# Leaving the last freed ring slot's load to the next block

## The chip, the cores and the metric

One core of a Trainium2 chip runs the whole program in one launch. The metric is the device time of one execution in microseconds (us). The kernel before took 2956.96 us (median of 3 runs, 2953.3 to 2957.9). Engines are called as in the profile: PE (TensorE matmuls), PEld (TensorE weight loads), DVE (VectorE), ACT (ScalarE), POOL (GpSimd), SP (SyncE). A "q" behind a name means the engine's sequencer: waits, branches, semaphore clears and the issue of DMAs.

## The reference

Two transformer blocks, one behind the other, on x of 256 tokens by 1024 channels, all in float32:

```python
def reference(x, ...):
    x = first_block(x, ...)      # 2 layers: token mixing, then a dense SwiGLU or a mixture of 8 experts
    return second_block(x, ...)  # RWKV-7 + NSA + S5 mixer, convolved FFN, per-layer embedding

def first_block(x, ...):
    for l in range(2):
        x = x + token_mixing(x, ...)          # rmsnorm, x @ w_in, pooling / mLSTM / FoX branches, gates, @ w_out
        h = rmsnorm(x, ffn_norm_g[l])
        x = x + (swiglu(h, ...) if l == 0 else moe_swiglu(h, ...))   # moe: top 2 of 8, 3584 wide
    return rmsnorm(x, final_norm_g)

def second_block(x, p, ...):
    z = rms_norm(h, ...) @ w_in
    mix = concat([rwkv7(z), nsa(z), s5(z)]) @ w_out
    h = h + rms_norm(mix); h = h + rms_norm(conv_ffn(rms_norm(h)))
    return h + sigmoid(h @ w_ple_gate) * rms_norm(p @ w_ple)
```

What matters for this change is only that nearly every product has a weight that is read once from memory, some 530 MB in all, and that the products come in a fixed order.

## The kernel before, in words

**The weight ring.** All big weights are cut into slabs of at most 128 partitions by 4096 floats (2 MB) and listed in `m.plan` in the order in which PE will use them (`plan_slabs`, `plan_experts`, `plan_second`, L183 to L222 and L1169). They pass through a ring of six slots in on-chip memory (`self.slots` is 6; a seventh slot of the tile serves as scratch). Slab i goes into slot i mod 6, so it can be loaded once PE is done with slab i - 6. PE counts the slabs it is done with in the semaphore `slabs_used`: `done_with_slab` (L155) notes a debt, and the next matmul without a signal of its own (L164), or `settle` at the end of the block (L173), pays it. `settle` first waits for the block's last matmul.

**Who loads.** Only SP issues slab loads (`issue`, L135, the DMA is L141). It works through them in order, and for slab i waits until `slabs_used` has reached i - 5. In Python, `self.used` is the number of slabs released up to the point that the program text has reached, and `self.issued` the number of slabs whose load is already written out. Nearly every block's SP program is `m.prefetch(sp)` (L144): issue up to slab `used + 6`, then clear the semaphores that the block before this one used (`clear_last`, L118; the clears are L120). The two pools of semaphores take turns from block to block.

**Blocks.** The program is a row of 51 such blocks, each one `nc.Block()` with a program for each engine. A block ends for all engines together: each drains, POOL gathers them, and releases them all into the next block. In the trace these are the DRAIN and EVENT_SEMAPHORE instructions on the line of the `with nc.Block()` that follows (L405 rmsnorm, L448 projections, L638 local mixers, L783 mLSTM, L898 attention, L999 merge, L1051 gated FFN, L1349 experts, L1592 extra jobs, L2215 NSA projections). The drain stands on the line of the block that ends. Where the SP program is written below the PE program (`rmsnorm`, `projections`, `local_mixers`, `merge`, `gated_ffn`, `experts`, `nsa_project` and others) `self.used` already counts the block's own slabs when `prefetch` is written out; so SP's last wait in such a block is for PE's last release.

**Blocks with loads of their own.** Some blocks have small loads on SP besides the ring. In `rwkv_prepare` (L1766 to L1770), `route`, `nsa_compressed`, `S5.prepare` and `ple` they stand ahead of `m.prefetch(sp)`. In `extra_jobs` (L1594 to L1606), which follows `experts` directly, `m.prefetch(sp)` stands first, and then a loop of as many rounds as a value computed on the chip says (one round here) waits and loads three tiles of 512 KB for PE (gate and up L1604, down L1606).

Of the kernel before, what the change touches and what calls it, by code (L numbers as in the profile page):

```python
# [50 lines left out]
class Signal:  # L51

    def __init__(self, sem):
        self.sem, self.n = sem, 0
# [23 lines left out]
class Machine:  # L79

    def __init__(self, nc, a, ctx):
        self.nc, self.a, self.ctx = nc, a, ctx
        self.names = {}
        self.slots = SLOTS - 1
        sem = lambda name: ctx.enter_context(nc.semaphore(name))
        self.slab_in = [sem(f"slab_in{i}") for i in range(SLOTS)]
        self.slabs_used = sem("slabs_used")
        self.load_in = [sem(f"load_in{i}") for i in range(6)]
        self.pools = [[sem(f"phase{b}_{i}") for i in range(26)] for b in (0, 1)]  # L90
        self.turn = 0
        self.taken = 0
        self.dirty = [0, 0]
        self.plan = []
        self.number = {}
        self.issued = 0
        self.used = 0
        self.owed = 0
        self.ring = self.sb("ring", [P, SLOTS, SLAB])
        self.bank = [ctx.enter_context(nc.psum_tensor(f"bank{i}", [P, 512], F32)) for i in range(8)]  # L100

# [13 lines left out]
    def sem(self):  # L115
        return self.signals(1)[0].sem
# [5 lines left out]
    def end_block(self):  # L122
        self.dirty[self.turn] = self.taken
        self.turn, self.taken = 1 - self.turn, 0

    def add_slab(self, key, src, kt, n):
# [15 lines left out]

    def prefetch(self, sp):  # L144

        self.issue(sp, self.used + self.slots)
        self.clear_last(sp)

    def slab(self, pe, key):
# [2678 lines left out]
```

## Time and profile before

| | |
|---|---|
| runs | 2956.96 us median (2953.3, 2956.96, 2957.9) |
| the profiled execution | 2956.46 us, of which 2954.7 us is the span from the first to the last instruction |
| PE busy | 2548.4 us, 86% of the span |
| PEld / DVE / ACT / POOL busy | 1751.8 / 688.2 / 271.2 / 75.6 us |
| mean granted TensorE clock | 0.903 of full speed |
| memory traffic | 529.67 MB read, mean 181 GB/s |

The profile is of one execution. Busy time is the time in which an engine works, sequencer instructions left out. A row of a timeline gives start, length, engine, line and operation; rows for one line of the source give the number of instructions, their shortest, median and longest duration in ns, and the start of the first and the last.

### The profile page before, as it was taken

The page shows a single profiled execution, that of the slowest core. Times are in us where ns is not written, and L with a number is a line of the kernel's source. Part 1 is how long each engine was busy: PE and PEld are TensorE (multiplying, and loading weights), DVE is VectorE, ACT ScalarE, POOL GpSimd, SP SyncE. Part 2 cuts the span into 40 slices and gives each one's busy share as a digit, 9 for nine tenths or more (in the row PEclk, how much of TensorE's full clock was granted, in tenths as well). Part 3 has the DMA queues.
Part 4 walks back from the last instruction along what each step waited for, and adds up shares of the span by engine and source line. Part 5 has one row for each costly group of instructions (what it writes and reads, how often), then busy time and mean ns, then how long its engine had stood idle before and what let it go on. Part 6 is the DMA issues. An engine that isn't in the chain of part 4 may idle for free. (4 is left out here: it accounts for less than half of the span.)

```text
span 2954.7 us, 43386 instructions
## 1 busy us (share of the span) xinstructions
PE 2548.4 (86%) x19584; PEld 1751.8 (59%) x19584; DVE 688.2 (23%) x1523; ACT 271.2 (9%) x510; POOL 75.6 (3%) x139
## 2 busy tenths in 40 slices
PE   5988989989989899999999999984576755779976
PEld 4766778877667745345354354443475643468865
DVE  1322310013222210101001000112374224533332
ACT  0222100001222010000000000001100001110000
POOL 1000000000000000000000000001000003100000
PEclk9988999999889989999999999997786855889987
DMA  6321424353311649999999999990200310014320
GB/s 223 141 71 43 159 98 171 114 186 118 113 45 46 225 174 382 372 393 389 367 406 374 370 407 373 378 364 22 92 1 1 124 34 0 11 47 171 128 75 15
DMA packets 165222, 533.51 MB, mean 181 GB/s; under 512 B 16012, under 2 KB 31278, under 8 KB 148654
## 3 DMA queue, kind: packets, MB, share of 16 engines
q1 hardware_dynamic: 158944, 529.86, 48.0%
q8 instruction: 154, 2.52, 0.3%
q10 hardware_dynamic: 6094, 0.88, 0.2%
q14 instruction: 30, 0.25, 0.0%
HBM read 529.67 MB, written 1.05 MB: 180 GB/s over the span
## 5 line engine op out<-in xcount | busy, mean ns | idle before, releaser
L160 PE MATMUL bank<-hT,ring 128*128 128x256 f32 x3280 | 752.4, 390 | 55.1 <-PEq L405 23.6
L160 PEld LDWEIGHTS bank<-hT,ring 128*128 128x128 f32 x3280 | 639.6, 196 | 156.8 <-issue 64.7
L160 PE MATMUL bank<-ring,moe_he 128*32 128x512 f32 (+1 forms) x6144 | 579.6, 539 | 0.0
L160 PEld LDWEIGHTS bank<-ring,moe_he 128*32 128x32 f32 x6144 | 199.2, 110 | 375.3 <-issue 373.8
L160 PE MATMUL bank<-ring,moe_actT 128*32 128x256 f32 x5376 | 293.2, 379 | 0.0
L160 PEld LDWEIGHTS bank<-ring,moe_actT 128*32 128x32 f32 x5376 | 174.0, 110 | 116.6 <-issue 3.4
L1552 DVE TENSOR_TENSOR moe_act<-moe_silu,bank 128x512 f32<-128x512 f32 (+1 forms) x48 | 26.9, 616 | 547.6 <-PE bank L160 547.6
L160 PE MATMUL bank<-norm_sq,ones 128*128 128x256 f32 x160 | 58.8, 547 | 51.5 <-ACT norm_sq L408 51.5
L160 PEld LDWEIGHTS bank<-norm_sq,ones 128*128 128x128 f32 x160 | 45.0, 289 | 65.2 <-ACT norm_sq L408 55.4
L160 PE MATMUL bank<-cffn_act,ring 128*128 128x256 f32 x352 | 79.7, 379 | 0.4 <-DVE cffn_act L1151 0.4
L160 PE MATMUL bank<-ffn_act,ring 128*128 128x256 f32 x352 | 79.4, 379 | 0.0
L160 PEld LDWEIGHTS bank<-cffn_act,ring 128*128 128x128 f32 x352 | 66.8, 190 | 9.8 <-DVE cffn_act L1151 0.8
L160 PEld LDWEIGHTS bank<-ffn_act,ring 128*128 128x128 f32 x352 | 66.9, 190 | 9.1
L160 PE MATMUL bank<-ring,hT 128*128 128x512 f32 (+1 forms) x192 | 67.8, 513 | 2.2 <-PEq L448 2.2
L1485 ACT ACTIVATE moe_silu<-bank 128x512 f32<-128x512 f32 (+1 forms) x48 | 22.6, 545 | 415.1 <-PE bank L160 415.1
L1116 DVE TENSOR_TENSOR ffn_act<-ffn_gate,bank 128x256 f32<-128x256 f32 x22 | 9.3, 421 | 216.1 <-ACT ffn_gate L1112 216.1
L160 PE MATMUL bank<-merged,ring 128*128 128x256 f32 x256 | 55.7, 380 | 3.0 <-PEq L999 3.0
L160 PEld LDWEIGHTS bank<-merged,ring 128*128 128x128 f32 x256 | 48.5, 190 | 10.3 <-issue 3.8
L1512 DVE TENSOR_TENSOR xT<-xT,bank 128x512 f32<-128x512 f32 x32 | 19.8, 681 | 147.5 <-PE bank L160 147.5
L160 PEld LDWEIGHTS bank<-ring,hT 128*128 128x128 f32 x192 | 33.2, 201 | 34.9 <-issue 34.9
L1145 DVE TENSOR_SCALAR cffn_cgate<-bank,param 128x256 f32<-128x256 f32 x22 | 12.0, 543 | 147.8 <-PE bank L160 147.8
L1502 DVE COPY moe_ye<-bank 128x256 f32<-128x256 f32 x8 | 3.4, 424 | 152.1 <-PE bank L160 152.1
(595 smaller groups left out, 2168.5 us busy)
## 6 DMA issues: line engine op xcount, KB each, us to landing
ring<-in_moe_w_down SPq DMA_DIRECT2D x56, 2048.0 KB, 14.0
ring<-in_moe_w_gate SPq DMA_DIRECT2D x32, 2048.0 KB, 16.7
ring<-in_moe_w_up SPq DMA_DIRECT2D x32, 2048.0 KB, 9.8
ring<-in_w_in SPq DMA_DIRECT2D x29, 2048.0 KB, 8.0
ring<-in_moe_w_gate SPq DMA_DIRECT2D x32, 1536.0 KB, 8.2
ring<-in_moe_w_up SPq DMA_DIRECT2D x32, 1536.0 KB, 8.5
ring<-in_w_up SPq DMA_DIRECT2D x10, 2048.0 KB, 7.9
ring<-in_w_out SPq DMA_DIRECT2D x6, 2048.0 KB, 7.8
```

Source lines behind the costliest of these rows:

```text
L160: ins = pe.matmul(out, lhsT, rhs, start=start, stop=stop, **kw)
L1116: v.tensor_tensor(act, gate, bank[:, T:2 * T], ALU.mult).then_inc(sg["act"].sem, 1)
L1145: k.step(v.tensor_scalar(to, hu, tap(2, row), bias(row), ALU.mult, ALU.add))
L1485: act.activation(x.sg[:, g, 0:32 * nb], G[g][:, 0:32 * nb], ACT.Silu).then_inc(sg_ready.sem, 1)
L1502: v.tensor_copy(x.ye[:, 2, :], DN[1][:, 0:T]).then_inc(ye_ready.sem, 1)
L1512: ins = v.tensor_tensor(m.xT[:, 2 * cg:2 * cg + 2, :], m.xT[:, 2 * cg:2 * cg + 2, :], SC[cg][:].rearrange("p (c n) -> p c n", c=2), ALU.add)
L1552: v.tensor_tensor(x.act[:, g, 0:32 * nb], x.sg[:, g, 0:32 * nb], U[g][:, 0:32 * nb], ALU.mult)\
```

## The change

`end_block` notes how many slabs had been released when the block ended (`began` for the next one). `prefetch` no longer issues up to `used + 6`: it stops at `used + 5`, but never short of `began + 6`. So a block that releases u slabs (u at least 1) leaves the load that waits for the last of these releases to the next block, whose SP program starts with it; a block that releases none issues all that is open, as before. Where the plan has no more slabs, nothing changes.

```diff
@@ Machine.__init__
         self.owed = 0
+        self.began = 0
@@
     def end_block(self):
         self.dirty[self.turn] = self.taken
         self.turn, self.taken = 1 - self.turn, 0
+        self.began = self.used
@@
     def prefetch(self, sp):
 
-        self.issue(sp, self.used + self.slots)
+        self.issue(sp, max(self.began + self.slots, self.used + self.slots - 1))
         self.clear_last(sp)
```

## Rows read from the trace of the kernel before

**Rows 1.** The profile's page: busy us of each engine, share of the span, instructions

```profile
PE 2548.4 (86%) x19584; PEld 1751.8 (59%) x19584; DVE 688.2 (23%) x1523; ACT 271.2 (9%) x510; POOL 75.6 (3%) x139
```

**Rows 2.** The waits, of SP's queue and of PE: total, times, longest

```profile
SPq L141 <- PE bank L160: 1907.2, 259, 34.7
...
PE bank L1621 <- DMA ring<-in_moe_w_down: 3.2, 1, 3.2
```

**Rows 3.** Line L448 from 380 to 402 us: how a block of projections ends

```profile
L448 DVEq DRAIN  x1: 783/783/783, 400.4 to 400.4; - x1
...
L448 SPq DRAIN  x1: 7/7/7, 401.1 to 401.1; - x1
```

**Rows 4.** The timeline around the same end

```profile
400.38 0.75 DVE L623 TENSOR_TENSOR xT<-xT,bank 128x256 f32<-128x256 f32 x2 [6.16 <-PE bank L160]
400.46 0.37 SPq L141 DMA_DIRECT2D ring<-in_ff_w_down  x1
401.43 1.91 ACT L408 ACTIVATE norm_sq<-xT 128x2048 f32<-128x2048 f32 x1 [65.10 <-PEq L448]
```

**Rows 5.** The timeline from 2594.5 us, and L120 there: the second output projection's end

```profile
2595.07 0.76 DVE L2139 COPY hT<-bank 128x256 f32<-128x256 f32 x2 [6.15 <-PE bank L160]
2595.15 0.37 SPq L141 DMA_DIRECT2D ring<-in_w_down  x1
2596.54 1.91 ACT L408 ACTIVATE norm_sq<-hT 128x2048 f32<-128x2048 f32 x1 [30.46 <-PEq L448]
...
L120 SPq EVENT_SEMAPHORE_RANGE_CLEAR  x15: 25/25/25, 2595.6 to 2596.6; - x15
```

**Rows 6.** The timeline from 2337 us: the end of the NSA projections

```profile
2337.91 0.42 DVE L2174 COPY s_u<-bank 128x256 f32<-128x256 f32 x1 [3.03 <-PE bank L160]
...
2338.99 0.20 POOL L2265 MEMSET swap<- 128x128 f32 x1 [282.73 <-POOLq L2215]
```

**Rows 7.** The timeline from 132.5 us: the end of the local mixers

```profile
133.32 0.60 ACT L695 ACTIVATE fq<-bank 128x512 f32<-128x512 f32 x1 [6.31 <-PE bank L160]
...
134.22 0.68 DVE L787 TENSOR_TENSOR_SCAN run_max<-gi 4x256 f32<-4x256 f32 x1 [10.28 <-PEq L638]
```

**Rows 8.** SP's timeline around attention and merge; the page's landing times

```profile
305.63 0.37 SPq L141 DMA_DIRECT2D ring<-in_w_br_ml  x1
329.98 0.37 SPq L141 DMA_DIRECT2D ring<-in_w_br_fox  x1
336.89 7.28 SPq L141 DMA_DIRECT2D ring<-in_w_out  x2
...
ring<-in_w_in SPq DMA_DIRECT2D x29, 2048.0 KB, 8.0
```

**Rows 9.** The timeline from 1984 us: experts' end and the extra job

```profile
1985.44 0.37 SPq L141 DMA_DIRECT2D ring<-in_w_in  x1
1987.67 2.48 DVE L1512 TENSOR_TENSOR xT<-xT,bank 128x512 f32<-128x512 f32 x4 [3.08 <-PE bank L160]
...
1994.90 1.55 SPq L1604 DMA_DIRECT2D hT<-in_moe_w_up  x1
1996.68 0.39 SPq L1606 DMA_DIRECT2D ring<-in_moe_w_down  x1
...
2002.58 3.84 PE L1621 MATMUL bank<-moe_silu,hT 128*128 128x128 f32 x32 [3.19 <-DMA ring<-in_moe_w_down]
```

**Rows 10.** DMA rate from 1986 to 2004 us, in 40 slices of 0.45 us

```profile
GB/s 0 109 164 305 396 400 400 419 400 419 405 396 396 360 109 0 0 0 0 0 36 97 242 313 346 196 139 270 216 215 376 411 421 191 46 18 0 0 0 0
```

**Rows 11.** rwkv_prepare: the slabs before it, its last small load (L1769), its first matmuls

```profile
2094.40 6.93 SPq L141 DMA_DIRECT2D ring<-in_w_out  x2
...
L1769 SPq DMA_DIRECT2D rw_g<-in_rw_g x1: 577/577/577, 2103.2 to 2103.2; - x1
...
DMA to landing us min/median/max: 6.8/6.8/6.8
...
L1849 PE MATMUL bank<-rw_shifted,rw_w2a x6: 631/631/763, 2112.0 to 2114.2; 64*128 64x256 f32 x6
```

## The prediction

> **What bounds the kernel now.** I read the page first: PE is busy 2548.4 us (86% of the span) [rows 1]. So loads matter only where PE waits for one. The waits say where that is: SP waited 259 times, 1907.2 us in all, for PE to release slabs [rows 2]. The ring is full most of the time and the loads run ahead; no row has PE waiting for a slab of the ring. PE waits for a load only in four blocks with small loads of their own; the one that touches this change is the extra job's, 3.2 us before L1621 [rows 2]. So the change can't help PE to its weights. It can act on two things: when SP reaches the end of a block, and what stands in the DMA queue early in the next one. I went through both, block by block, in the timeline and in the drains.
>
> **What is removed.** Eighteen blocks release slabs. In one of them, the convolved FFN, the plan of slabs runs out before the block ends, so 17 are changed. In each, SP now waits for PE's last release, issues the load (0.37 us), clears 2 to 20 semaphores at 25 ns each, some 0.06 us from one to the next [rows 5], and drains. From now on it clears and drains long before. That is worth the time by which SP is the last at the gathering, and no more.
>
> The typical end is the first layer's output projection [rows 4]: PE's last matmul starts DVE's last two copies at 400.38 and, 0.08 us later, SP's load. DVE is through after 0.75 us and its drain, from 400.4 over 783 ns, ends at 401.18; SP, with 0.37 us for the load and four clears, drains at 401.1 [rows 3]. DVE is last, by some 0.07 us, and the next block's ACT starts at 401.43 [rows 4], 0.30 us behind DVE's last copy. Taking SP away moves nothing. By the same reading, in seven of the 17 ends SP is ahead by 0.01 to 0.11 us (three first projections, two output projections, two merges), and in six by 1.8 us and more (mLSTM and attention in both layers, dense FFN, experts). Worth zero each; the cover is DVE's tail.
>
> Four are left. At the second block's output projection SP has 13 clears (15 from 2595.6 on, two of them the next block's). DVE is done at 2595.07 + 0.76 = 2595.83, the next block's ACT starts at 2596.54 [rows 5]: 0.71 us, against 0.30 where DVE is last. Gain 0.41. The NSA projections: DVE done at 2338.33, POOL starts at 2338.99 [rows 6], 0.66 us, so 0.36. The local mixers, in both layers: ACT done at 133.92, DVE starts at 134.22 [rows 7], 0.30 us, so nothing to 0.02. **Together -0.8 us**, and no more than 0.1 us off, since what is late next, DVE's drain, is seen in the same rows.
>
> **What is moved: the load.** It is issued behind the barrier instead of before it, 1 to 24 us later. Six slots mean that PE has five more slabs ahead of it. The tightest place is attention into merge, where the release lies mid-block and slabs go fast: the load issued at 305.63 moves to the start of merge, some 0.6 us before its next issue at 329.98, so 329.4, and merge consumes a slab in 6.9 us (329.98 to 336.89) [rows 8]. PE wants this one four slabs on, at about 329.4 + 27.6 = 357. A slab of twice its size lands 8.0 us after issue [rows 8], so at the latest at 337.4. Cover 19 us; elsewhere 60 us and more. **Zero.** In `rwkv_prepare` three small loads now go ahead of the slab instead of behind it. They landed at 2103.2 + 6.8 = 2110.0, and PE's first matmul there came at 2112.0 [rows 11], 2 us later, so their earlier arrival is worth nothing.
>
> **The extra job.** Here the slab comes first and the critical loads stand behind it. Now: last slab issued 1985.44, experts ends with DVE at 1990.15, job loads issued from 1994.4 to 1996.68, PE starts at 2002.58 when the down tile has landed [rows 9]. The rate shows the slab's data from about 1986.5 to 1992.8, five empty slices, and the job's 1.57 MB from 1995.0 to 2002.2 [rows 10]. After: the slab is issued at 1990.4, its data shift by 5.0 us and end near 1997.7; SP comes to its job loads 0.42 us later (one issue of 0.37 and its gap). The queue serves in order: in `rwkv_prepare` the small load issued at 2103.2 lands at 2110.0 [rows 11], about 1 us behind the slab issued at 2094.40 + 6.93 - 0.37 = 2100.96, which by the median of 8.0 [rows 8] lands at 2109.0. So the job's data start at 1997.7. How long they take then is not shown. From below: at the slab's own 400 GB/s, 3.9 us, landing at 2002.0: -0.5 us. From above: as long as now, 7.2 us, landing at 2005.2: +2.7. Now they have a dip to 139 GB/s, while the up tile's issue took 1.55 us [rows 9, 10]; a backlog hides that. Without the dip: 1.05 MB of gate and up at about 313 GB/s, 3.35 us, and 0.52 MB of down at 400, 1.3 us, so 2002.7. With SP's 0.42 us partly on top I take **+0.6 us**, near the lower end, since the rate is measured on these loads. PE, ACT and DVE follow in one chain to the end of that block, so all of it counts.
>
> Gate and up are cut from memory in pieces of 128 floats, 512 B (the slices of L1596), and move at 242 to 346 GB/s where the slab has 400 [rows 10]. The Trainium skill (DMA: Bandwidth & Descriptors, Specifications) says that transfers from 512 B on reach line rate; by that the job's data would be through in about 4 us and the term would be nearly 0 instead of +0.6. The trace shows 512 B clearly slower, and the sum goes by it.
>
> **Sum.** -0.8 + 0.6 = -0.2 us. Against the profiled execution's own 2956.46 that is 2956.3; the median of the runs is 0.5 above it, so **2956.7 us**. Ends of the sum: -1.3 and +1.9.
>
> **Rivals.**
> - *The extra job's loads get in the slab's way (slower).* If slab and job loads share the engines, or SP's issue of up blocks until the slab is drained, the last landing moves by the slab's whole shift, +5.0 us; PE already waits 3.2 us there, so there is no cover and it decides from the first 0.1 us. Net +4.2: 2961.2. For it: the up tile's issue was held once already. Against: the five empty slices [rows 10] show that the engines have room, and the order of landing [rows 11] that what is queued behind a slab follows it closely.
> - *Every end gets shorter (faster).* If SP's late load held the gathering in all 17 blocks, each would give 0.37 us and four clears, 0.6 us: -10 us, 2946.5. Against: DVE's drain ends behind SP's in 13 of them.
> - *It does nothing that PE sees*: SP's part of an end and the later slab are both hidden, 2957.0. It lies within the forecast's range and is counted there.
> - *The clock falls otherwise.* All that follows moves by fractions of a us, and TensorE's clock may be granted a little earlier or later. Whatever it does from run to run lies within the spread of the three runs of before, -3.7 to +0.9 us of their median; I take that as its price.
>
> **The numbers.** The forecast, between -1.3 and +1.9: 0.82. The extra job's rival 0.09, every end shorter 0.03, the clock or something unseen 0.06. About 0.2%, 5.9 us, is what a measurement of this kernel can tell from no change. All cases but the second rival lie within it; for the tails I leave 0.03 faster and 0.05 slower. Range: 2956.96 - 1.3 - 3.7 = 2952.0 to the first rival's 2961.2.
>
> **What would show it.** Right: SP's drain long before DVE's at all 17 ends; at the two ends named, next engine 0.30 us behind DVE; a slab load as SP's first instruction in the block behind each; PE's wait before L1621 at 3.2 + 0.6 us. Wrong: any PE wait for the ring, above all early in merge; L1621 more than 2 us later behind experts' end; a stretch without slabs that is longer or shorter by over 1 us.

## The result and the profile after

The changed kernel takes 2961.37 us (median of 20 runs, 2959.56 to 2962.75), the kernel before 2955.61 us (20 runs on the same chips, 2952.45 to 2957.9). The ratio is 1.0020, 95% interval 1.0013 to 1.0027: **5.8 us slower** (3.8 to 8.0). The forecast of 2956.7 us was wrong, and the time lies just outside its range.

The profiled execution of the changed kernel took 2961.22 us, span 2959.5, against 2956.46 and 2954.7 before. From the old L141 on, every line has a number two higher (L141 is now L143, L1621 is L1623). I went through both profiles block by block. The page says first that PE is busy longer with the same number of matmuls [rows 1]:

```profile
PE 2552.3 (86%) x19584; PEld 1754.8 (59%) x19584; DVE 688.8 (23%) x1523; ACT 271.2 (9%) x510; POOL 75.6 (3%) x139
```

The same work took PE 3.9 us more, so matmuls ran at another clock somewhere. The other engines' sums hardly moved.

**The ends of blocks.** Three answers of the profile after: the drains of the first layer's output projection, and the timelines of the second output projection's end and of the NSA projections' end (start, length, engine, line, operation).

```profile
L450 SPq DRAIN  x1: 7/7/7, 388.9 to 388.9; - x1
L450 DVEq DRAIN  x1: 783/783/783, 401.7 to 401.7; - x1
```

```profile
2599.78 0.76 DVE L2141 COPY hT<-bank 128x256 f32<-128x256 f32 x2 [6.15 <-PE bank L162]
2600.81 0.37 SPq L143 DMA_DIRECT2D ring<-in_w_down  x1
2600.83 1.91 ACT L410 ACTIVATE norm_sq<-hT 128x2048 f32<-128x2048 f32 x1 [30.05 <-PEq L450]
...
2342.67 0.42 DVE L2176 COPY s_u<-bank 128x256 f32<-128x256 f32 x1 [3.03 <-PE bank L162]
...
2343.38 0.20 POOL L2267 MEMSET swap<- 128x128 f32 x1 [282.43 <-POOLq L2217]
...
2343.39 0.37 SPq L143 DMA_DIRECT2D ring<-in_w_up  x1
```

SP now drains at 388.9, some 13 us ahead of DVE, where it was 0.07 us ahead [rows 3]. At the second output projection ACT starts 0.29 us behind DVE's last copy (2599.78 + 0.76 to 2600.83); it was 0.71 [rows 5]. At the NSA projections POOL starts 0.29 us behind DVE (2343.09 to 2343.38); it was 0.66 [rows 6]. In each block behind, a slab is SP's first load.

**The late slab.** SP's timeline around attention and merge, where it was tightest:

```profile
330.56 0.37 SPq L143 DMA_DIRECT2D ring<-in_w_br_ml  x1
331.30 0.37 SPq L143 DMA_DIRECT2D ring<-in_w_br_fox  x1
338.21 0.37 SPq L143 DMA_DIRECT2D ring<-in_w_out  x1
```

The load issued at 305.63 before [rows 8] is now merge's first, and no PE wait for it follows. PE still waits for loads in only four places, and the ring's slabs are in none of them; the one that touches the change has grown from 3.2 to 4.7 us [rows 2]. PE's waits, the last two of the four lines with a DMA as releaser (total, times, longest):

```profile
PE bank L1276 <- DMA route_w<-in_moe_w_router: 8.1, 1, 8.1
PE bank L1623 <- DMA ring<-in_moe_w_down: 4.7, 1, 4.7
```

**The extra job** is where the time went. Its timeline after, and the rate of all loads from 1987 us on in 40 slices of 0.55 us, against [rows 9, 10]:

```profile
1988.99 2.48 DVE L1514 TENSOR_TENSOR xT<-xT,bank 128x512 f32<-128x512 f32 x4 [3.08 <-PE bank L162]
1991.76 0.37 SPq L143 DMA_DIRECT2D ring<-in_w_in  x1
...
1996.12 0.40 SPq L1606 DMA_DIRECT2D hT<-in_moe_w_gate  x1
1996.61 0.60 SPq L1606 DMA_DIRECT2D hT<-in_moe_w_up  x1
1997.44 2.76 SPq L1608 DMA_DIRECT2D ring<-in_moe_w_down  x1
2005.44 5.44 PE L1623 MATMUL bank<-moe_silu,hT 128*128 128x128 f32 x32 [4.73 <-DMA ring<-in_moe_w_down]
```

```profile
GB/s 6 0 0 0 0 0 0 0 0 0 71 93 313 384 413 410 413 402 384 413 399 341 287 312 305 296 290 342 373 338 95 30 15 0 0 0 0 0 0 0
```

The slab's 2.10 MB fill the slices from 1992.5 to about 1998.75, and the job's 1.57 MB follow without a gap. They end with the slices at 2003.5 to 2005.15 (95, 30, 15 GB/s), and PE starts at 2005.44. It did this 12.43 us behind DVE's last addition before (2002.58 - 1990.15) and does it 13.97 us behind it now. From here on **landing** is the time from the end of the experts' block (0.06 us behind DVE's last addition) until the down tile is in (0.04 us ahead of PE's start): 12.33 us before, 13.87 after.

And the 32 products themselves take 5.44 us instead of 3.84 [rows 9]. The stretches of those products, after and before (length, then busy us of PE, PEld, DVE, ACT and POOL, mean granted clock, DMA share, GB/s):

```profile
2005.40:2011.00 5.60, 5.44 (x32) 5.25 (x32) 0.00 (x0) 0.08 (x1) 0.00 (x0) 0.70 0.00 0
```

```profile
2002.50:2006.50 4.00, 3.84 (x32) 3.65 (x32) 0.00 (x0) 0.05 (x1) 0.00 (x0) 1.00 0.00 0
```

```profile
1991.53:2021.02 29.49, 16.52 (x84) 14.07 (x84) 3.69 (x8) 2.45 (x5) 0.00 (x0) 0.83 0.39 125
2021.02:2035.56 14.54, 6.71 (x16) 5.07 (x16) 5.01 (x9) 3.67 (x3) 0.00 (x0) 0.67 0.00 0
2035.56:2049.66 14.10, 6.27 (x16) 4.78 (x16) 5.01 (x9) 2.38 (x2) 0.00 (x0) 0.62 0.00 0
```

```profile
1990.20:2016.55 26.35, 14.91 (x84) 12.46 (x84) 3.69 (x8) 2.45 (x5) 0.00 (x0) 0.87 0.28 93
2016.55:2030.95 14.40, 6.57 (x16) 4.97 (x16) 5.01 (x9) 3.67 (x3) 0.00 (x0) 0.66 0.00 0
2030.95:2044.98 14.03, 6.20 (x16) 4.73 (x16) 5.01 (x9) 2.38 (x2) 0.00 (x0) 0.62 0.00 0
```

The block grew by 3.14 us: 1.54 by landing and 1.60 by the clock. The two behind it grew by 0.21. That is +3.35 of the +4.8 us between the two executions. Another +1.3 are in the first blocks, whose end lies at 1990.2 before and 1991.5 after. That is scatter: another execution of the kernel before has it at 1992.6.

**Behind the three blocks** the two executions are equally long to the end of the span: 909.7 us before (2954.7 - 2044.98), 909.8 after (2959.5 - 2049.66). Two ends in there are 0.79 us shorter (0.42 and 0.37), so the rest of that stretch took as much longer. A good part of it lies behind the second output projection. The stretches from ACT's start there to the end of the span, in the kernel before, in a second execution of it (below: "before, once more") and in the changed kernel:

```profile
2596.54:2954.70 358.16, 298.41 (x1300) 257.51 (x1300) 119.05 (x233) 25.73 (x35) 0.00 (x0) 0.90 0.24 86
2599.14:2955.90 356.76, 296.75 (x1300) 256.06 (x1300) 119.12 (x233) 25.74 (x35) 0.00 (x0) 0.91 0.24 86
2600.83:2959.50 358.67, 298.81 (x1300) 257.74 (x1300) 119.13 (x233) 25.73 (x35) 0.00 (x0) 0.90 0.24 86
```

The difference is PE's busy time. Between the second row and the third the largest part of it is in the last rmsnorm. Its 16 matmuls took 3.72 us at a granted clock of 1.00 in that second execution of before and 6.62 us at 0.62 in the changed kernel; in the first execution of before they took 6.62 us too:

```profile
2896.76:2902.95 6.19, 3.72 (x16) 2.96 (x16) 0.00 (x0) 2.38 (x2) 0.00 (x0) 1.00 0.00 0
2898.67:2907.76 9.09, 6.62 (x16) 5.04 (x16) 0.00 (x0) 2.38 (x2) 0.00 (x0) 0.62 0.00 0
```

### The profile page after: what moved, and what is told of

It is laid out like the page before. It is cut to its first block and busy times, and to the rows that moved or that the text cites. A ratio compares the mean times of both kernels' runs of the same rounds, so it can differ in the third digit from the quotient of the medians.

```text
span 2959.5 us, 43386 instructions
## 1 busy us (share of the span) xinstructions
PE 2552.3 (86%) x19584; PEld 1754.8 (59%) x19584; DVE 688.8 (23%) x1523; ACT 271.2 (9%) x510; POOL 75.6 (3%) x139
## 5 line engine op out<-in xcount | busy, mean ns | idle before, releaser
L1554 DVE TENSOR_TENSOR moe_act<-moe_silu,bank 128x512 f32<-128x512 f32 (+1 forms) x48 | 26.9, 616 | 547.6 <-PE bank L162 547.6
```

What stands on the lines that cost most here:

```text
L1554: v.tensor_tensor(x.act[:, g, 0:32 * nb], x.sg[:, g, 0:32 * nb], U[g][:, 0:32 * nb], ALU.mult)\
```

## The experiments

**My theory** at this point: the slab, now ahead of the job's three loads in SP's queue, delays the down tile; PE stands still longer; its clock falls for the products. **Rivals:** the slab that comes late everywhere costs time in places no wait shows; the clock falls anyway, from run to run; SP, not the queue, is what delays the job's loads.

Eleven kernels ran, three of them repeats. This table has what each profile showed, in us; "products" are the 32 matmuls of L1621 (the granted clock beside them where I read it), "rms" the two rmsnorm blocks together. With the 8 idle matmuls PE doesn't wait for the tile, and its landing is that of the load itself.

| kernel | landing | PE's wait | products | job's block | rms | sum |
|---|---|---|---|---|---|---|
| before | 12.33 | 3.19 | 3.84 (1.00) | 26.35 | 28.43 | 54.78 |
| before, once more | 12.67 | 3.54 | 5.47 (0.69) | 28.32 | 26.87 | 55.19 |
| after | 13.87 | 4.73 | 5.44 (0.70) | 29.49 | 28.64 | 58.13 |
| after, once more | 13.97 | 4.82 | 5.39 | 29.54 | 28.61 | 58.15 |
| experts whole | 11.53 | 2.40 | 3.84 | 25.55 | 26.47 | 52.02 |
| experts short | 14.00 | 4.87 | 5.37 | 29.55 | 28.58 | 58.13 |
| slab behind the job | 11.06 | 1.91 | 3.84 | 25.07 | 26.80 | 51.87 |
| the same again | 11.07 | 1.91 | 3.84 | 25.08 | 26.81 | 51.89 |
| clears behind the job | 11.05 | 1.92 | 3.84 | 25.07 | 26.80 | 51.87 |
| slab ahead, clears behind | 13.98 | 4.83 | 5.38 | 29.53 | 28.59 | 58.12 |
| 28 more clears | 12.89 | 3.75 | 5.46 | 28.54 | 26.77 | 55.31 |
| 8 idle matmuls | 14.21 | 0 | 3.73 | 29.77 | 28.44 | 58.21 |
| 4 idle matmuls | 13.99 | 1.42 | 3.84 (1.00) | 28.00 | 27.19 | 55.19 |

**Experts whole.** The changed kernel, but the experts' block keeps its last load. Everything else of the change stays.

```diff
-    def prefetch(self, sp):
-        self.issue(sp, max(self.began + self.slots, self.used + self.slots - 1))
+    def prefetch(self, sp, full=False):
+        self.issue(sp, self.used + self.slots if full else max(self.began + self.slots, self.used + self.slots - 1))
@@ the experts' block @@
-            m.prefetch(sp)
+            m.prefetch(sp, True)
```

> The changed kernel, but the experts block issues up to used + 6 again, so that nothing is left for the extra job's block; the other 16 ends stay changed. Theory A (the extra job's block carries the loss: its loads stand behind the slab, and PE's longer wait also costs TensorE's clock): that block is back at 26.35 us from the experts' end to its own, PE's wait before the job's gate and up products at 3.2 us, those products at 3.84 us; only the two shorter ends are left, so 0.8 us under the kernel before, ratio 0.9997. Theory B (the 16 other late loads cost something somewhere, too): 2 to 5 us above the kernel before, ratio 1.001 to 1.002, with blocks elsewhere longer.

Measured: 2957.02 us against 2956.18 (ratio 1.0006, 0.9997 to 1.0015), and 4.35 us below the changed kernel. The job's loads are as before, without the slab between:

```profile
1995.07 0.53 SPq L1606 DMA_DIRECT2D hT<-in_moe_w_up  x1
...
2001.94 3.84 PE L1623 MATMUL bank<-moe_silu,hT 128*128 128x128 f32 x32 [2.40 <-DMA ring<-in_moe_w_down]
```

Most of the loss is gone with this one load back in its place. What the change does in the other 16 blocks can't be told from nothing: the interval reaches from -0.9 to +4.4 us. The expected gain of 0.8 us didn't show; the median is 0.8 above the kernel before, which would fit the longer stretch behind the second output projection (358.8 us here).

**Experts short.** The other half alone: the kernel before, with only the experts' block one slab short.

```diff
-    def prefetch(self, sp):
-        self.issue(sp, self.used + self.slots)
+    def prefetch(self, sp, short=0):
+        self.issue(sp, self.used + self.slots - short)
@@ the experts' block @@
-            m.prefetch(sp)
+            m.prefetch(sp, 1)
```

> The kernel before, with one part of the change: the experts block alone stops one slab short, and the extra job's block begins with that load. Theory A: its block 29.5 us instead of 26.35, of which 1.5 us is PE's longer wait (4.7 instead of 3.2 us) and 1.6 us the gate and up products at half the granted clock (5.4 instead of 3.84 us); 3.1 us above the kernel before, ratio 1.0011. Theory B: less than half of the changed kernel's 5.8 us, and the rest is missing here; if it is all of the 5.8 us, the job's block costs more than the two profiles show.

Measured: 2960.17 against 2956.18 (1.0015, 1.0006 to 1.0024), +4.0 us. The row is that of the changed kernel:

```profile
2005.53 5.37 PE L1621 MATMUL bank<-moe_silu,hT 128*128 128x128 f32 x32 [4.87 <-DMA ring<-in_moe_w_down]
```

The two halves, +0.8 and +4.0, make up 4.8 of the 5.8. One block holds most of the loss, and the first rival falls as the main cause; that the other blocks cost about 1 us isn't excluded.

**Slab behind the job.** The changed kernel, with SP's `prefetch` behind the job's three loads.

```diff
         def _(sp):
-            m.prefetch(sp)
...
                 sp.dma_start(wd, down[...]).then_inc(w_in.sem, 16)
+            m.prefetch(sp)
```

> The changed kernel, but in the extra job's block the SP program's prefetch (the owed slab and the semaphore clears) stands behind the job's loads. Theory A: no slab ahead of the loads and 18 clears less, 1.4 us; the down tile lands 1.4 us sooner than in the kernel before, PE's wait before L1623 is 1.8 us or less, the clock holds, the block some 25 us; with the two shorter ends 2.2 us under the kernel before, ratio 0.9993. Theory B: at or above the kernel before, since the other late loads are still there.

Measured: 2953.61 against 2956.18 (0.9995, 0.9986 to 1.0004). The job's loads go first and land 2.8 us earlier than in the changed kernel:

```profile
1995.41 0.51 SPq L1607 DMA_DIRECT2D ring<-in_moe_w_down  x1
1996.18 0.38 SPq L143 DMA_DIRECT2D ring<-in_w_in  x1
2002.16 3.84 PE L1623 MATMUL bank<-moe_silu,hT 128*128 128x128 f32 x32 [1.91 <-DMA ring<-in_moe_w_down]
```

So the order in the queue is the cause, as far as this run can tell: the clears moved behind the loads with the slab, and "slab ahead, clears behind" below separates the two. A landing 2.8 us sooner made the three blocks 6.3 us shorter (58.13 to 51.87), more than twice as much.

**Clears behind the job.** "Experts whole" with the same move, so that only the clears of semaphores stand behind the job's loads and no slab does.

```diff
@@ the experts' block @@
-            m.prefetch(sp)
+            m.prefetch(sp, True)
@@ the extra job @@
         def _(sp):
-            m.prefetch(sp)
...
                 sp.dma_start(wd, down[...]).then_inc(w_in.sem, 16)
+            m.prefetch(sp)
```

> As the first of these (experts issues its last slab itself), and in the extra job's block the clears stand behind the job's loads. Theory A: the same as the run with slab and clears behind the loads, 2.2 us under the kernel before, ratio 0.9993; the slab lands before the block begins. If the run with the slab behind the loads is slower than this one by over 1 us, the late slab costs something after the job as well.

Measured: 2953.72 against 2956.18 (0.9995, 0.9986 to 1.0004). Landing, at 11.05, and the three blocks equal those of "slab behind the job" to 0.01 us. A slab behind the job's loads costs them nothing.

**The kernel before, once more**, unchanged: how typical was the one execution that I had read?

> The kernel before once more, for a second profile. If the experts-only and the all-but-experts kernels' profiles tell of the chip and not of the edit, the first two blocks differ here too by some tenths of a us from the first profile with the same program, and the job's landing lies between 11.5 and 12.4 us behind the experts' end; the extra job and the two rmsnorm blocks behind it together are then either near 52 or near 55 us.

It wasn't. This execution took 2957.62 us. The up tile's issue held SP for 1.77 us, landing was at 12.67, PE stood still for 3.54 us, and the products ran as in the changed kernel:

```profile
1997.31 1.77 SPq L1604 DMA_DIRECT2D hT<-in_moe_w_up  x1
...
2005.33 5.47 PE L1621 MATMUL bank<-moe_silu,hT 128*128 128x128 f32 x32 [3.54 <-DMA ring<-in_moe_w_down]
```

```profile
2005.30:2010.80 5.50, 5.47 (x32) 5.28 (x32) 0.00 (x0) 0.00 (x0) 0.00 (x0) 0.69 0.00 0
```

So the fallen clock isn't the slab's own doing; it stands behind a long standstill. The kernel before had it in one of its two profiles, and the changed order of loads in all four in which PE was given no extra work (the changed kernel twice, "experts short", "slab ahead, clears behind"). Beside this execution of before the changed kernel's products are no slower (5.44 against 5.47 us): its three blocks are 2.9 us longer by 1.2 of landing and 1.8 in the rmsnorm blocks.

**PE kept busy: 8 idle matmuls.** The changed kernel with eight matmuls, whose result nobody reads, between PE's gather and its wait for the job's weights.

```diff
                 ins.then_inc(gath.sem, 1)
+                for _ in range(8):
+                    pe.matmul(m.bank[6][:], m.ident[:], x.h_tok[:, 0, 0:512], start=True, stop=True)
                 pe.wait_ge(he_ready.sem, i + 1)
```

> The changed kernel, and in the extra job's block PE runs eight more matmuls (128 by 512, into a bank that nothing reads) between the gather and its wait for the job's weights; the extra matmuls change no result. Clock theory (1.6 of the 3.1 us of that block are TensorE's clock, which falls because PE stands still for 4.7 us): the weights still land some 13.9 us behind the experts' end, but the gate and up products take 3.84 us instead of 5.44; the block 27.9 instead of 29.5 us, and the two rmsnorm blocks behind it shorter or equal; 1.6 to 4 us under the changed kernel. Rival (the products are slower because the loads or the slab disturb them): they stay at 5.4 us and the time stays within 0.5 us of the changed kernel's.

A miss: 2961.58 against 2955.84 (1.0022, 1.0013 to 1.0031). The eight ran in 16 passes and took 7.0 us, past the landing:

```profile
2001.93 7.03 PE L1620 MATMUL bank<-ring,ident 128*128 128x512 f32 x16
```

The products took 3.73 us but began 1.7 us late, at 2008.80, which ate what the clock gave. It shows one thing: the rmsnorm blocks were long (28.44) although PE had neither stood still nor lost its clock before the products.

**PE kept busy: 4 idle matmuls**, the same edit with `range(4)`, so that they end ahead of the landing.

> The changed kernel with four extra matmuls ahead of PE's wait for the job's weights, instead of the eight that ran on past the landing (they change no result). Four are 3.5 us of PE work, from 9.0 to 12.6 us behind the experts' end, so that the weights, at 13.9 us, end the wait again. Clock theory: products in 3.8 us instead of 5.4, the job's block 27.9 us instead of 29.5. Whether the two rmsnorm blocks behind it are at 28.6 or at 26.6 us together is open; the time is 1.6 us under the changed kernel in the one case, 3.6 in the other. Rival: products at 5.4 us in spite of them, and no gain.

Measured: 2957.82 against 2955.59 (1.0007, 0.9998 to 1.0016), 3.5 us below the changed kernel run beside it (2961.36, below).

```profile
1999.19 3.60 PE L1620 MATMUL bank<-ring,ident 128*128 128x512 f32 x8
...
2004.21 3.84 PE L1625 MATMUL bank<-moe_silu,hT 128*128 128x128 f32 x32 [1.42 <-DMA ring<-in_moe_w_down]
```

```profile
2004.20:2008.10 3.90, 3.84 (x32) 3.65 (x32) 0.00 (x0) 0.02 (x1) 0.00 (x0) 1.00 0.00 0
```

Landing is at 13.99 as in the changed kernel, and only PE's standstill is shorter, 1.42 us. The clock is 1.00, the block 1.54 us shorter and the rmsnorm blocks 1.42. So filling the standstill gave back 3.0 us in the profile and 3.5 in the medians without moving the landing. The 1.54 in the products is the clock's answer to the standstill. For the 1.42 in the rmsnorm blocks this isn't shown: with 8 idle matmuls they stayed long.

**28 more clears.** The kernel before, with SP held up ahead of the job's loads. Does a late SP do the same without a slab?

```diff
             m.prefetch(sp)
+            for s in (m.pools[1 - m.turn][:14] * 2):
+                sp.sem_clear(s)
```

> The kernel before, and in the extra job's block SP clears semaphores 28 times more ahead of the job's loads: a delay of 1.54 us, with no slab in the queue. Clock theory: the down tile lands 13.9 us behind the experts' end, the gate and up products take 5.4 us, the block is 29.5 us; so 3.1 us over the kernel before, as with the slab. Rival (the slab itself disturbs the products): products 3.84 us, the block 27.9 us, +1.5 us.

Measured: 2956.22 against 2955.84 (1.0003, 0.9994 to 1.0013). A half miss: SP was 1.54 us later, but landing moved only to 12.89, where I had expected 13.9, because the up tile's issue wasn't held this time:

```profile
1998.43 0.53 SPq L1606 DMA_DIRECT2D hT<-in_moe_w_up  x1
1999.20 0.75 SPq L1608 DMA_DIRECT2D ring<-in_moe_w_down  x1
2005.13 5.46 PE L1623 MATMUL bank<-moe_silu,hT 128*128 128x128 f32 x32 [3.75 <-DMA ring<-in_moe_w_down]
```

PE's wait of 3.75 us brought the products at the lower clock, with no slab in the queue. The time can't be told from that of the kernel before.

**Slab ahead, clears behind.** The changed kernel with the slab first, but the 18 clears behind the job's loads. If SP is the limit, the tile lands sooner; if the queue is, it doesn't.

```diff
         def _(sp):
-            m.prefetch(sp)
+            m.issue(sp, m.began + m.slots)
...
                 sp.dma_start(wd, down[...]).then_inc(w_in.sem, 16)
+            m.clear_last(sp)
```

> The changed kernel, but in the extra job's block only the owed slab stands ahead of the job's loads; the 18 clears stand behind them, so that SP issues the job's loads 1.4 us sooner. If the queue is the limit (the slab's data first, then the job's 1.57 MB at their own rate): the down tile still lands 13.6 to 13.9 us behind the experts' end, the block stays at 29.5 us, the time at the changed kernel's. If SP's issue is the limit: landing 12.4 us, products at full clock, block 26.4 us, 3.1 us under the changed kernel.

Measured: 2961.61 against 2955.84 (1.0020, 1.0011 to 1.0029).

```profile
1992.54 0.37 SPq L143 DMA_DIRECT2D ring<-in_w_in  x1
1995.61 0.40 SPq L1606 DMA_DIRECT2D hT<-in_moe_w_gate  x1
...
1997.25 3.88 SPq L1608 DMA_DIRECT2D ring<-in_moe_w_down  x1
2006.33 5.38 PE L1624 MATMUL bank<-moe_silu,hT 128*128 128x128 f32 x32 [4.83 <-DMA ring<-in_moe_w_down]
```

The gate tile goes out 3.07 us behind the slab instead of 4.36 (1996.12 - 1991.76), and landing stays at 13.98. SP's lead is spent in the down tile's issue, 3.88 us instead of 2.76. Against "slab behind the job", from which it differs only in the slab's place, the tile lands 2.92 us later. The queue is the limit, and the rival of SP falls.

**Two repeats**, of the changed kernel and of "slab behind the job", on one chip.

> The changed kernel once more. Landing 13.8 to 14.1 us behind the experts' end in this profile, too, the job's block 29.5 us, the two rmsnorm blocks behind it 28.6 us; 5 to 6 us above the kernel before (ratio 1.0018 to 1.0020). If its block is below 28 us here, the loss is not carried by it.

> The changed kernel with the job's block's slab and clears behind its loads, once more, for more runs. From the first time: 2953.6 us, 2.5 us under the kernel before (ratio 0.9992), 7.7 under the changed one; the down tile lands 11.1 us behind the experts' end, the job's block 25.1 us. If the landing is what decides, nearly all runs lie close together, under 2956 us, while those of the kernel before spread over 6 us.

Measured, against 2955.59: the changed kernel 2961.36 (1.0017, 1.0008 to 1.0026), slab behind the job 2954.28 (0.9995, 0.9986 to 1.0004). Both profiles repeat the landing and the three blocks of the first ones within 0.1 us. "Slab behind the job" is 7.1 us under the changed kernel. It may be 1 to 2.5 us under the kernel before, and so may "clears behind the job", but the intervals of all three hold no difference, so a version that beats both kernels isn't shown. Its spread came as expected: 2952.85 to 2955.91 us in its 11 runs, against 2951.78 to 2959.37 in 27 of the kernel before.

## Why the prediction was wrong

- **Where SP was last: right at the ends, but the time didn't get through.** -0.41 and -0.36 us were forecast and -0.42 and -0.37 came, and the local mixers gave 0.01 each. The rival of shorter ends everywhere is out. But the term of -0.8 us took it for granted that what an end gives reaches the end of the kernel. Behind the three blocks the nine executions with the shorter ends took 909.1 to 909.8 us, and the four with the old ends 909.7, 908.1, 907.9 and 908.6. The changed kernel's own two have 909.8: nothing of the 0.8 us is left.
- **The late slab costs no wait: right**, at attention and everywhere else, by the missing waits.
- **What the queue does: right.** The job's data were to start 7.5 us behind the experts' end and started 7.2 behind it (1998.75 - 1991.53). Their main part was to take 4.65 us and took 4.75.
- **The step that failed** is the +0.6 us of the extra job. It has two faults. One is arithmetic of the landing: I counted bytes at 313 and 400 GB/s and let PE start some 0.35 us behind them, but the loads end in a tail, three slices of 95, 30 and 15 GB/s, 1.65 us, and PE starts 0.3 us behind it. The kernel before had the tail too (191, 46, 18 GB/s, then 0.4 us to PE [rows 9, 10]), so it was there to be read. Landing was therefore +1.5 us, inside my bounds of -0.5 to +2.7, where I took +0.6 near the lower end. (My own terms don't quite give +0.6 either: 2002.7 is 0.1 behind 2002.58, and SP's 0.42 whole on top makes 0.5.)
- **The larger fault** is that I took that block at its landing and made the clock a rival of its own, worth no more than the spread of the runs. It is a consequence of the same wait: against the execution that the forecast started from it costs 1.60 us in the products, and 4 idle matmuls in the wait gave 3.5 us of the run back. How much of the rmsnorm blocks' share belongs to it isn't shown. The clock was in the rows as a risk that goes with the wait, and the sum should have carried it in one term with the landing.
- **I took one execution of the kernel before for the kernel.** Its landing was 12.33, and with the same order of loads there were 11.53 and 12.67 as well. The sum of the three blocks is 51.9 to 52.0 with a landing up to 11.5, 54.8 to 55.3 from 12.3 to 12.9, and 58.1 to 58.2 from 13.9 on, unless PE is given work. Both profiles of the kernel before are in the second; the first showed in "experts whole", with before's order of loads. That the kernel before moves between the two is not shown, but would fit runs that reach down to 2952.45 and up to 2957.9. The changed kernel was in the third in both profiles, and its lowest run, 2959.56, is above the highest of before. If it is so, the change didn't add a fixed price, and its price depends on which execution of before stands beside it.
- **The rival on the slow side** had the sign right and the mechanism wrong: landing was to move by the whole +5.0 us, and it moved by 1.5, with the clock doing the rest. That its 2961.2 is near the result is chance.

**How far the 5.8 us is explained.** The medians of the two half kernels put the price of the slab ahead of the job's loads at 4.0 us ("experts short" less before) and 4.35 (after less "experts whole"). In the profiles the three blocks are 2.9 to 3.4 us longer than in the two executions of before, and 6.1 longer than in "experts whole". There is a second place: the stretch from the second output projection's end to the end of the span. It took 356.2 to 358.2 us in the four executions with the old ends (before twice, "experts short", "28 more clears") and 358.6 to 358.9 in all nine with the shorter ones. There the changed kernel loses 0.5 to 2.6 us, more than the 0.42 that the end ahead of it gives. That the shorter ends bring this on is not shown: the first execution of before has nearly the long form with the old ends, and no run changed these ends alone. Together, the three blocks and all that follows them are 3.5 us longer after than in the first execution of before and 4.7 longer than in the second. The first blocks, whose end moves by up to 2.4 us from one execution of the same kernel to the next, make up the rest between single executions. What stays open is how often the kernel before runs in each of these forms, and with it 1.1 to 2.3 us of the 5.8, which itself has an interval of 3.8 to 8.0.

In the job's block the granted clock was down behind PE's longer standstills (3.54 to 4.87 us) and not behind the shorter ones (1.42 to 3.19). The Trainium skill (TensorE: Matmul & The Clock Gate, Part 1: The HAM clock gate) says of the clock that "the default state is throttled, and activity releases the throttle". The trace agrees in the products: 0.70 behind a standstill of 4.73 us, 1.00 when four matmuls left 1.42 us of it. By that rule the price would have belonged in the term of the wait. What sets the clock in the rmsnorm blocks stays open: they were long (28.4 to 28.6 us) behind products at 1.00 in the kernel before and with 8 idle matmuls, and short (26.8, 26.9) behind products at the lower clock in two others. No run separated what decides that, nor what decides the clock of the rmsnorm blocks near the end of the kernel.

The gate and up tiles, cut into pieces of 512 B, moved at 287 to 373 GB/s here, right behind a slab at 384 to 413. That is again below the line rate that the Trainium skill (DMA: Bandwidth & Descriptors, Specifications) gives from 512 B on. The measurement decides, and here it also says that this part of my sum wasn't the one that failed.

## What to carry to other kernels

Before you defer a prefetch to the next block, look at what that block loads for itself: in one queue the deferred load goes ahead of loads that somebody is waiting for, and it belongs behind them. Cost the wait that grows together with the clock of the matmuls behind it, since 1.2 to 1.5 us more of standstill went with three blocks that were 2.9 to 3.4 us longer here. Don't count what a shorter block end gives as a gain of the whole kernel until the blocks behind it have been read. And read a landing, its tail included, in several executions of the kernel before you call it its landing.

## What the runs showed of the hardware

- An issue on SP can be held when loads are outstanding ahead of it. The down tile's took 0.39 us [rows 9] where little was queued, 2.76 with a slab and two tiles ahead, and 3.88 when it came sooner. Without the slab the up tile's varied from 0.37 and 0.53 to 1.55 and 1.77 us between executions. SP's busy time says nothing of when the data land.
- The loads end in a tail that no division of bytes by a rate contains: three slices of 0.55 us at 95, 30 and 15 GB/s after, three of 0.45 us at 191, 46 and 18 before [rows 10].
- A matmul of 128x512 f32 appears as two passes, 16 for 8 matmuls, 0.44 us each (7.03 / 16). Idle matmuls that are to bridge a wait have to be counted that way.
